# Routed experts through a DRAM scratch: seven of eight outputs scattered by row with indirect DMAs, read back during the eighth; start, choice and end put in another order

## What is computed

```
logits = (h @ router_w)                       # 256 x 8
top_val, top_idx = lax.top_k(logits, 2)
gates = sum(one_hot(top_idx) * softmax(top_val))
for e in range(8):                            # expert e: 1024 -> 2816 -> 1024
    y = y + gates[:, e] * (silu(h @ w_gate[e]) * (h @ w_up[e])) @ w_down[e]
x = x + y
return rms_norm(x, ln_final)
```

## Time and profile before

| | |
|---|---|
| median of three runs | 1190.61 us |
| the profiled execution: its own time | 1190.02 us |
| its span (first to last instruction) | 1188.0 us |
| mean granted TensorE clock | 0.997 of full speed |
| moved by DMA | 344.6 MB, 290 GB/s over the span |

### The profile page before, as it was taken

The page is one execution under the profiler, slowest core; times in us unless marked ns, Lnnn a source line. Parts: engine busy times, 40 slices in busy tenths (PEclk is TensorE's granted clock), DMA queues, the critical chain, the costliest instruction groups (busy, mean ns, idle before and its releaser), DMA issues.

```text
span 1188.0 us, 18370 instructions
## 1 busy us (share of the span) xinstructions
PE 1167.3 (98%) x6010; PEld 981.9 (83%) x6010; DVE 975.7 (82%) x1101; ACT 828.6 (70%) x1007; POOL 30.9 (3%) x43
## 2 busy tenths in 40 slices
PE   7999999999999999999999999999999999999996
PEld 7997888888998788888888888888888888888885
DVE  4867555545675999999899999989999989999996
ACT  6655554534653788878778778868887877887884
POOL 0400000000120000000000000000000000000000
PEclk9999999999999999999999999999999999999999
DMA  9955655556444399999899999989999999999960
GB/s 284 370 182 164 196 192 194 177 183 207 142 161 142 109 376 364 395 342 368 330 338 369 372 373 360 355 331 347 362 396 342 361 336 338 375 365 368 366 238 35
DMA packets 142614, 344.64 MB, mean 290 GB/s; under 512 B 6112, under 2 KB 64688, under 8 KB 142528
## 3 DMA queue, kind: packets, MB, share of 16 engines
q1 hardware_dynamic: 141952, 342.34, 80.3%
q0 software_dynamic: 352, 1.09, 0.4%
q10 hardware_dynamic: 224, 0.10, 0.1%
HBM read 342.06 MB, written 1.44 MB: 289 GB/s over the span
## 4 chain that ended last, share of the span: by engine, by line
PE 91%; DVE 4%; ACT 2%; DMA 2%; issue 1%; SPq 0%; DVEq 0%; ACTq 0%
PE psum L1144 87%; PE psum L1141 4%; DMA raw<-in_w_in 1%; DVE prob L900 1%; DVE w_lo L381 0%; DVE smax L884 0%; DVE score L880 0%; ACT w_hi L372 0%; DMA skew<-bias_rows 0%; DVE nmax L885 0%; ACT aT_hi L590 0%; DVE x_sb L828 0%; ACT squares L578 0%; ACT aT_hi L726 0%; ACT w_hi L392 0%
## 5 line engine op out<-in xcount | busy, mean ns | idle before, releaser
L399 DVE TENSOR_TENSOR w_lo<-raw,w_hi 128x1024 fp32r<-128x1024 f32 x528 | 627.3, 1220 | 40.9 <-PE psum L1144 15.7
L392 ACT ACTIVATE w_hi<-raw 128x1024 fp32r<-128x1024 f32 x528 | 550.2, 1061 | 110.1 <-PE psum L1144 108.3
L1144 PE MATMUL psum<-w_hi,aT_hi 128*128 128x512 f32 (+1 forms) x1232 | 447.2, 372 | 1.4 <-ACT w_hi L372 0.6
L1144 PE MATMUL psum<-w_hi,aT_lo 128*128 128x512 f32 (+1 forms) x1232 | 440.0, 366 | 0.0
L1144 PE MATMUL psum<-w_lo,aT_hi 128*128 128x512 f32 (+1 forms) x1232 | 323.3, 366 | 0.8 <-DVE w_lo L381 0.7
L1144 PEld LDWEIGHTS psum<-w_hi,aT_hi 128*128 128x128 f32 x1232 | 233.4, 189 | 38.6 <-issue 1.8
L1144 PEld LDWEIGHTS psum<-w_hi,aT_lo 128*128 128x128 f32 x1232 | 233.6, 190 | 35.0
L1144 PEld LDWEIGHTS psum<-w_lo,aT_hi 128*128 128x128 f32 x1232 | 214.6, 189 | 40.4 <-DVE w_lo L399 1.8
L381 DVE TENSOR_TENSOR w_lo<-raw,w_hi 128x1024 fp32r<-128x1024 f32 x118 | 144.8, 1234 | 48.7 <-PE psum L1144 44.6
L372 ACT ACTIVATE w_hi<-raw 128x1024 fp32r<-128x1024 f32 x118 | 124.6, 1059 | 82.4 <-PE psum L1144 74.2
L1144 PE MATMUL psum<-w_hi,heT_hi 128*128 128x512 f32 x352 | 138.1, 392 | 0.0
(11 more groups left out here) (179 smaller groups left out, 638.5 us busy)
## 6 DMA issues: line engine op xcount, KB each, us to landing
raw<-in_exp_w_down SPq DMA_DIRECT2D x88, 1024.0 KB, 7.1
raw<-in_exp_w_gate SPq DMA_DIRECT2D x80, 1024.0 KB, 7.0
raw<-in_exp_w_up SPq DMA_DIRECT2D x80, 1024.0 KB, 6.9
raw<-in_w_in SPq DMA_DIRECT2D x17, 1024.0 KB, 5.4
raw<-in_ffn_w_gate SPq DMA_DIRECT2D x22, 512.0 KB, 4.0
raw<-in_ffn_w_up SPq DMA_DIRECT2D x22, 512.0 KB, 5.1
raw<-in_ffn_w_down SPq DMA_DIRECT2D x11, 1024.0 KB, 5.0
raw<-in_w_out SPq DMA_DIRECT2D x8, 1024.0 KB, 8.1
```

Of the source, the lines that this page charges most:

```text
L392: nc.scalar.activation(w_hi[:, q % HIGHS, :], raw_piece(slot, q % 2), ACT.Copy).then_inc(hi_made, 1)
L399: eng.tensor_tensor(w_lo[:, q % LOWS, :], raw_piece(e_slot[q // 2], q % 2), w_hi[:, q % HIGHS, :].bitcast(F32), ALU.subtract).then_inc(lo_ ...
L1144: return pe.matmul(dst, a, b, start=start, stop=stop, skip_group_check=True)
```

## The change

1. **Seven outputs to DRAM.** ScalarE scales the output of experts 0 to 6 by the gate of each slot while copying it into `oe`; GpSimd writes it with an indirect DMA into rows of `scratch` (1024 rows of 4 KB), 0 to 511 in the first pass: a token's first choice at row t, its second at 256 + t. Unused slots get a row beyond the bound and are skipped. The row, gate and `rstd` of each slot come from one product with `info` (3 columns where `rstd` alone had 1), now after the second piece of a pair's first expert. `pick` is transposed, `put` made and `spread_out` run for expert 7 alone.
2. **Back.** After the seventh scatter has landed, GpSimd loads four blocks of 128 rows, one after the other, into `back` (which lies where `oe` lies); VectorE adds them to `x_sb` at pieces 10, 18, 26 and 34 of expert 7, each 128 x 1024.
3. **Clearing.** All 1024 rows of `scratch` are first written with zeros: two DMAs of 2 MB from a DRAM input `zeros`, issued by GpSimd. They stand in the source at step 5 of layer 0, but no wait stands ahead of them in GpSimd's program.
4. **Start.** Loads in the order x (half 0), first half of unit 0, x (half 1), second half of unit 0; `gain_rows` moves to ScalarE's queue; TensorE makes 8 and 6 products of zeros, turns the second half of x after the first piece; the bias rows come after the second piece, into banks 0 and 1.
5. **Choice and first expert.** 10 and 5 products in `keep_busy` for 8 and 3; `gather` goes tile by tile; ScalarE's first three pieces and table load and VectorE's first two `gather_low` and first piece are ahead of the gates and `info`.
6. **End.** The last two down pieces are made half by half (`last_two`), and squares, root and factor are taken once for all tokens after four half-row sums.

```diff
+ROWS = 2 * SEQ
+NO_ROW = 4096.0
+BACK = {10: 0, 18: 1, 26: 2, 34: 3}
@@ gpsimd, front
+                    if layer == 0 and s == 5:
+                        for r in range(2):
+                            pool.dma_start(scratch[r * ROWS:(r + 1) * ROWS, :], zeros).then_inc(scratch_cleared, 16)
@@ gpsimd, experts
+            def scatter_pass(r):
+                for e in range(LAST):
+                    v, j = e // 2, e % 2
+                    pool.wait_ge(rstd_e_made, N_PAIRS * r + v + 1)
+                    pool.wait_ge(oe_made, 2 * LAST * r + (2 * e + 2))
+                    pool.indirect_dma_start(scratch, bass.IndirectOffsetOnAxis(ap=row_e[:, v % 2, j:j + 1], axis=0), oe[:], None,
+                                            bounds_check=2 * ROWS - 1, oob_is_err=False).then_inc(scattered, 16)
+                pool.wait_ge(scattered, 16 * LAST * r + 16 * LAST)
+                for m in range(4):
+                    if m > 0:
+                        pool.wait_ge(back_added, 4 * r + m)
+                    pool.dma_start(back[:], rows[4 * r + m, :, :]).then_inc(back_landed, 16)
@@ scalar
+            def output_scaled(r, e):
+                act.wait_ge(piece_used, FFN_PIECES * (N_EXPERTS * r + e) + (FRONT_PIECES + FFN_PIECES))
+                if e > 0:
+                    act.wait_ge(scattered, 16 * LAST * r + 16 * e)
                 for b in range(2):
+                    nc.scalar.activation(oe[:, 512 * b:512 * (b + 1)], bank(6 + b), ACT.Copy,
+                                         scale=info_e[:, v % 2, j, 1:2]).then_inc(oe_made, 1)
@@ vector
+            for b in range(2):
+                gather_low(0, b)
+            low_part_e(dve, 0, 0)
...
+            def add_back(r, m):
+                dve.wait_ge(back_landed, 64 * r + 16 * (m + 1))
+                xs = x_sb[:, m % 2, :]
+                dve.tensor_tensor(xs, back[:], xs, ALU.add).then_inc(back_added, 1)
@@ tensor, in tensor_expert
-                    if e > 0 and q == 3:
-                        spread_out(i - 1, v)
+                    if j == 0 and q == 1:
+                        gather_info(r, e)
...
-                    if q == PICK_TURN:
+                    if e == LAST and q == PICK_TURN:
@@ tensor, front
-                    if layer == 0 and s == 0:
+                    if layer == 0 and s == 1:
 
                         pe.wait_ge(rows_ready, 1)
```

More of the change, by code:

```diff
@@ L446, in _ @@
                 if u == 0:
[L448 to L453 removed]
+                    continue
+                if kind == "in":
                     dst = raw[:, slot, :].rearrange("p (k n) -> p k n", k=DK)
@@ L597, in _ @@
                 n = 2 * layer
-                turned_high(n, range(4))
-                high(0 if layer == 0 else first - 1 + HIGHS)
+                if layer == 0:
+                    turned_high(n, range(2))
+                    high(0)
+                    turned_high(n, range(2, 4))
+                else:
+                    turned_high(n, range(4))
+                    high(first - 1 + HIGHS)
                 turned_high(n, range(4, DK))
@@ L738, in act_expert @@
                 i, v, j = N_EXPERTS * r + e, N_PAIRS * r + e // 2, e % 2
-                for q in range(HIGHS):
-                    if e == 0 and q == 2:
+                for q in range(EARLY if e == 0 else 0, HIGHS):
+                    if e == 0 and q == EARLY:
                         for b in range(4):
@@ L1069, in _ @@
             link(dve.tensor_tensor(tmp, hot2, wide(part2), ALU.mult))
-            for r in range(2):
-                link.also(dve.tensor_tensor(gatex[:, :, 8 * r:8 * r + 8], gates, tmp, ALU.add))
+            link.also(dve.tensor_tensor(info[:, :, :, 1], gates, tmp, ALU.add))
+            for t in range(TT):
+                step = link if t == TT - 1 else link.also
+                step(dve.tensor_scalar(rest[:, t, :], mask[:, t, :], cst[:, C_ROW + t:C_ROW + t + 1], None, ALU.mult))
+            link.also(dve.scalar_tensor_tensor(out=info[:, :, :, 2], in0=hot2, scalar=float(SEQ), in1=rest, op0=ALU.mult, op1=ALU.add))
+            link(dve.tensor_copy(info[:, :, :, 0], wide(rstd[:, 2, :])))
+            dve.tensor_copy(table_first[:], info[:, 0, 0, 0:1]).then_inc(info_ready, 1)
             dve.wait_ge(route_ready, 1)
@@ L1076, in vec_expert @@
                 i, v, j = N_EXPERTS * r + e, N_PAIRS * r + e // 2, e % 2
-                if e == 0:
-                    for b in range(2):
-                        gather_low(v, b)
-                for q in range(LOWS):
+                for q in range(1 if e == 0 else 0, LOWS):
                     low_part_e(dve, i, q)
-                if j == 0:
-                    rstd_low(v)
-                if e > 0:
-                    output_low(i - 1)
                 for q in range(FFN_PIECES):
-                    if e > 0 and q == 3:
-                        add_output(i - 1)
+                    if j == 0 and q == 3:
+                        slot_info(v, e // 2 % 2)
+                    if e == LAST and q in BACK:
+                        add_back(r, BACK[q])
                     for c in UP_WHOLE.get(q, ()):
@@ L1113, in _ @@
                 with dve.If(r > 0):
-                    dve.wait_ge(pick_turned, N_EXPERTS * r)
+                    dve.wait_ge(pick_turned, r)
+                    dve.tensor_scalar(info[:, :, :, 2], info[:, :, :, 2], float(ROWS), None, ALU.add).then_inc(info_ready, 1)
                     mark_slots(N_EXPERTS * r)
+                    for b in range(2):
+                        gather_low(N_PAIRS * r, b)
+                    low_part_e(dve, N_EXPERTS * r, 0)
                 with dve.Else():
@@ L1144, in mm, with turn_h @@
                 return pe.matmul(dst, a, b, start=start, stop=stop, skip_group_check=True)
-            def turn_h(n):
-                for half in range(2):
+            def turn_h(n, halves=range(2)):
+                for half in halves:
+                    if n == 0 and half == 0:
+                        pe.wait_ge(g_landed, 32)
+                        pe.matmul(psum[:, 7, 2 * REL:2 * REL + 4 * DK], gain_rows[:], ident[0:4 * DK, 0:4 * DK], is_transpose=True,
+                                  start=True, stop=True, skip_group_check=True).then_inc(gain_turned, 1)
                     if n == 0:
@@ L1440, in tensor_expert @@
                 for q in range(FFN_PIECES):
+                    if e == N_EXPERTS - 1 and q == FFN_PIECES - 2:
+                        last_two(i)
+                        break
                     if j == 0 and q in (0, 4, 6):
```

235 lines of the change are left out of this document (152 added, 83 removed).

## The result

The changed kernel takes **1194.62 us** (median of 5 runs, 1193.89 to 1196.62) where the kernel before takes 1190.61 (5 runs beside it, 1189.17 to 1190.88): a ratio of 1.0042, 95% interval 1.0028 to 1.0057. It is 0.4% slower, where 1181.5 us was forecast. Its profiled execution took 1196.11 us, 1194.3 of them inside the span (before: 1190.02 and 1188.0), so the two traces have 6.3 us between them to account for, where the medians have 4.0.

The account below looks back on a forecast made before the run. TensorE, 98% busy, was taken as the bound in the expert stage, DMA at the start. Terms -15.8 + 0 + 6 + 2.5 - 1.3 = -8.6 us, against 1190.0, gave 1181.5 us, range 1173 to 1192.

Parts of the forecast that it names:

- What it removes: Expert stage: seven spread_out runs, seven pairs of pick transposes and seven TensorE waits go; -15.8 us.
- The weight stream as the bound: Rival, expert stage: weight loads can't exceed 356 GB/s, so the 15.8 us gain is lost; 1197 us, chance 0.09.
- The clearing and the start: Start: clearing delays the first loads, unit 5 lands near 39.5 us, not 33.5; +6 us, bounds -1.5 and +12.
- Choice and first expert: First expert: VectorE's small operations make the second w_lo late for TensorE; +2.5 us, bounds 0 and +5.
- The return trip: Expert 7: last scatter and first block take 14.6 us, TensorE late only from 16.5; 0 us, bounds 0 and 6.
- The end: Kernel's end: half the last output ready sooner, one root and factor for all tokens; -1.3 us, bounds -2.5 and 0.

Follow-up runs that it names:

- e1_late: The changed kernel with both clearing transfers moved from the start to the beginning of the second layer; 1188.84 us.
- e13_turns: e1_late with the second half of x turned before the first piece instead of after it; 1183.62 us.
- e16_best_skew: e15_best with SyncE's skew write and bias reads one load later, so bias rows don't hold unit 4; 1177.56 us.
- e15_best: e13_turns with the first expert's low parts earlier and information product later, returns four pieces later, and SyncE's first half output ahead of ScalarE's; 1180.45 us.
- e5_skew: e1_late with SyncE's skew write and bias reads one load later, so bias rows don't hold unit 4; 1185.63 us.
- e18_after_warm: The changed kernel with 6 unread products after the gather and 8 ahead of the first expert's second piece; 1191.62 us.

## Why the prediction was wrong, step by step

**What it removes, -15.8 us: right.** A pair takes 189.69 us, 189.8 was forecast. 13.6 us are gained until the end of expert 6; the 2.3 for expert 7 are taken over from its neighbours, not measured apart. Together they are 15.9.

**The weight stream as the bound: fell.** No new wait stands inside a pair.

**The clearing and the start, +6 us: the step that failed.** It was +13.2, beyond my bound of +12 (the pick comes at 410.5 to 410.8 us in all three traces with this start). I read the right chain (bias rows, SyncE's queue, unit 5) and took 26, 32 and 39.5 us for its three points; they were 30.5, 35.7 and 45.1. Two things were missing. The first is what follows the landings. The landings themselves I had about right: x's second half at 17.8 us instead of the 9.5 of e1_late, the rest of the first unit at 21.8 instead of 10.8. But I gave the chain behind them only a part of that, and let unit 5 land 7.5 us after its issue, where it took 9.4 (9.2 before). The clearing costs by a threshold (2 MB 0.2 us, 4 MB 5.8 us of the time), and moving it away gave back 7.7 us at the pick. The second is a term that I never priced: I expected of the new order of the start nothing or a gain of up to 1.5 us, and did not look for a loss: it costs 4.9 to 5.5 us by itself. 3.4 of them at the pick (5.2 of the time) come from the turning of x's second half after the first piece (e13_turns), the rest from SyncE's hold of unit 4 behind bias rows that now come a piece later (e16_best_skew against e15_best: 2.9 us of the time, 4.8 at the pick). Singly the two edits give more than there was to give, so this split is rough. I had followed the moved transfers to what they delay, and not the moved instructions.

**Choice and first expert, +2.5 us: the mechanism was right, a term was missing.** At a clock of 1.00 (e5_skew) the stretch is 103.3 against 100.7, +2.6, and the wait for the second `w_lo` is there. But the stands let the clock fall in most traces, and that costs another 3.1. I had written that the added products fit in waits, and had not asked whether the waits that I added would themselves cost the clock. e18_after_warm shows that they did: 3.0 us less, with the clock at 1.00.

**The return trip, 0 us: mis-sized.** It was some 3, inside the bounds of 0 and 6. The indirect scatter is issued 2.2 us into the expert, not 1.5, and has landed 8.1 us after that, and the first block takes 7.1, against 5.8 for each and 1.5 for the indices: 17.7 us in all against 14.6. I had said that TensorE is late only from about 16.5 us on; a block that comes at 17.7 is later than that, and TensorE's stand begins at 18.5.

**The end, -1.3 us: given back.** It was +0.2. The halves save 1.1 us up to VectorE's last add (4.0 us behind TensorE's last product instead of 5.1), but one root for both tokens makes ScalarE's output as late as VectorE's, and all three output transfers are issued behind it: from VectorE's last two products to the end it is 5.7 us instead of 4.5.

The sum of what was measured, -15.9 + 13.2 + 5.7 + 3.1 + 0.2, is +6.3 us. With the clearing, the start, the first expert, the returns and the end repaired and the idle products added, the same idea gives 1176.0, 5.5 us under the forecast. That the clearing costs 7.7 us at the pick but 5.8 in the median time is no contradiction: the traced executions of the changed kernel and of e1_late are 8.3 us apart, one above and the other below its median. What stays open is what makes the executions of one kernel spread by 4 to 5 us (e1_late: 1186.22 to 1191.77). The clock of the first expert is a part of up to 3 us of it; the rest was not found, and it leaves 1 us of every comparison above undecided. What a second pass would cost was not tried.

## What to carry to other kernels

A transfer that nobody waits for is not free while the DMA engines are the bound: look for the hole in their share, count the bytes that fit it, and put the rest where the share is low, as here in the second layer. When instructions are moved at the start, follow each result to the queue that stands behind it, engine by engine. And price a new stand of TensorE twice, once for its length and once for the clock behind it; where it can't be avoided, products that nobody reads can hold the clock; here they took no time that the measurement shows.

## What was not expected of the hardware

- The clock in the first expert is not a fixed property of the program. Kernels with the same order there ran at a mean of 1.00, 0.93 or 0.86 over the same 25 us. In the changed kernel TensorE stands 1.5 and 2.8 us, and from 423 to 430 us its granted clock is near its lower level (1.2 GHz), 0.53 on average:

```profile
423.00:430.00 7.00, 7.00 (x23) 5.75 (x22) 5.83 (x10) 2.54 (x3) 0.00 (x0) 0.53 0.93 312
```

  With 14 products in those stands it was at the upper one (2.4 GHz) in both traces taken: the changed kernel is 3.0 us faster, and for the repaired one (medians 1.6 apart) the time doesn't tell. e5_skew and e15_best stayed at 1.00 without them.
- Two MB of DRAM-to-DRAM clearing beside a full stream of 1 KB runs cost 0.2 us, and four cost 5.8; cut in 2 KB runs they cost the same within the uncertainty. The 544 GB/s of the row from 6 to 9 us is no rate of the engines: its neighbours have 319 and 355, and over 3 to 18 us the mean is 387, against 328 in e1_late.
- An indirect scatter from the 512 KB of `oe` landed in 8.0 us (7.6 to 8.3) beside the weight stream, a plain transfer of 512 KB (`back`) in 6.4 (4.3 to 7.4), and GpSimd needed 1.32 us to issue it against 0.57. It moves only the slots in use. The queue of GpSimd's transfers, before and after (packets, MB, share of the span):

```profile
q0 software_dynamic: 352, 1.09, 0.4%
```

```profile
q0 software_dynamic: 2032, 9.23, 2.2%
```

  Of the 8.14 MB more, 4.19 are the clearing and 2.10 the four blocks that come back; 1.85 are left for seven scatters, some 0.26 MB or 64 rows each. So a scatter took longer than a plain transfer of twice its bytes.
